# First modulation stage: odd tiles of the adaptive weights go to TensorE, even tiles stay on VectorE; input and matrices are loaded in one run per partition, the matrices last

## The reference, cut to what matters

```python
mod = (jax.nn.silu(c.astype(jnp.float32)) @ ada_w[l].astype(jnp.float32)
       + ada_b[l].astype(jnp.float32))[:, None, :]
shift1, scale1, gate1, shift2, scale2, gate2 = jnp.split(mod, 6, axis=-1)

h = rms_norm(x, norm1_g[l]) * (1.0 + scale1) + shift1
z = (h.astype(in_dtype) @ w_in[l]).astype(jnp.float32)
```

## Time and profile before

| | |
|---|---|
| time, median of 3 executions | 2176.35 us (2171.0 to 2176.57) |
| the profiled execution | 2177.08 us |
| its span | 2175.2 us |
| TensorE (PE) busy | 1868.7 us, 86% |
| VectorE (DVE) busy | 1485.5 us, 68% |
| ScalarE (ACT) busy | 1016.9 us, 47% |
| GpSimd (POOL) busy | 437.7 us, 20% |
| mean granted TensorE clock | 0.94 |

### The profile page before, as it was taken

How to read it: one execution, slowest core, us unless ns; L and a number is a source line. 1 busy time by engine, 2 the same in 40 slices (tenths; PEclk the granted TensorE clock), 3 DMA queues, 4 the chain that set the end, 5 groups by cost and what they waited for, 6 DMA issues and landing times. The chain is left out here.

```text
span 2175.2 us, 33251 instructions
## 1 busy us (share of the span) xinstructions
PE 1868.7 (86%) x12082; PEld 1393.0 (64%) x12082; DVE 1485.5 (68%) x2609; ACT 1016.9 (47%) x2046; POOL 437.7 (20%) x457
## 2 busy tenths in 40 slices
PE   4974897878888778777799989889999999779998
PEld 4842887644432222222279988678998988668997
DVE  6675554777767667666466675766677787676666
ACT  2444212445544444444355554467665545335554
POOL 0010220045454434434200000002231330210000
PEclk8987998889999999999999999699999999889999
DMA  8861001399999999999955655035555655224553
GB/s 327 292 219 34 3 3 41 109 406 420 419 419 420 419 420 419 420 420 420 386 185 184 192 172 202 1 116 176 191 181 177 192 175 174 93 84 160 186 189 98
DMA packets 104385, 497.31 MB, mean 229 GB/s; under 512 B 11856, under 2 KB 17232, under 8 KB 71376
## 3 DMA queue, kind: packets, MB, share of 16 engines
q1 hardware_dynamic: 66064, 225.41, 31.2%
q0 software_dynamic: 36864, 268.45, 29.8%
q10 hardware_dynamic: 1344, 1.96, 0.3%
HBM read 494.73 MB, written 1.05 MB: 228 GB/s over the span
## 5 line engine op out<-in xcount | busy, mean ns | idle before, releaser
L247 PE MATMUL ps<-srcs,wh 128*128 128x512 f32 x2064 | 743.2, 402 | 32.1 <-DVE srcs L261 20.4
L1874 PE MATMUL ps<-row,diag 128*128 128x512 f32 x1024 | 502.3, 626 | 121.4 <-ACT diag L1957 121.2
L249 PE MATMUL ps<-srcs,wl 128*128 128x256 f32 x2064 | 583.5, 283 | 0.0
L229 DVE TENSOR_TENSOR wl<-ring,wh 128x1024 fp32r<-128x1024 f32 x362 | 452.3, 1252 | 123.0 <-ACT wh L223 121.8
L247 PEld LDWEIGHTS ps<-srcs,wh 128*128 128x128 f32 x2064 | 392.5, 190 | 127.7 <-issue 35.9
L1874 PEld LDWEIGHTS ps<-row,diag 128*128 128x128 f32 x1024 | 184.0, 195 | 430.1 <-ACT diag L1957 271.7
L2050 DVE CUSTOM_DVE_ANT_0 row<-row,h_tok 128x1024 f32<-128x1024 f32 x256 | 313.8, 1226 | 198.6 <-DMA row<-in_peer_uv,experts 190.7
L223 ACT ACTIVATE wh<-ring 128x1024 fp32r<-128x1024 f32 x362 | 379.1, 1052 | 66.3 <-PE ps L249 43.5
L249 PEld LDWEIGHTS ps<-srcs,wl 128*128 128x128 f32 x2064 | 396.3, 192 | 2.0 <-issue 1.9
L1811 POOL DMA_INDIRECT row<-in_peer_uv,experts x256 | 281.5, 1100 | 393.1 <-PE ps L1874 342.9
L1950 ACT ACTIVATE acts<-dots 128x1 f32<-128x1 f32 x256 | 51.8, 202 | 329.4 <-DVE dots L2050 328.9
(11 more groups left out here) (503 smaller groups left out, 2083.0 us busy)
## 6 DMA issues: line engine op xcount, KB each, us to landing
ring<-in_stream SPq DMA_DIRECT2D x378, 512.0 KB, 3.7
alpha<-in_ada_late SPq DMA_DIRECT2D x12, 512.0 KB, 5.1
beta<-in_ada_late SPq DMA_DIRECT2D x10, 512.0 KB, 6.0
kappa<-in_ada_late SPq DMA_DIRECT2D x10, 512.0 KB, 5.9
row<-in_peer_uv,experts POOLq DMA_INDIRECT x256, 15.4
bias<-in_attn_bias SPq DMA_DIRECT2D x8, 256.0 KB, 5.0
w<-in_cmp_w SPq DMA_DIRECT2D x1, 2048.0 KB, 7.5
xT<-in_xT SPq DMA_DIRECT2D x1, 1024.0 KB, 15.9
```

The source lines that it names most:

```text
L229: nc.vector.tensor_tensor(wl[:, n % PAIRS, :], ring[:, tile % RING, :], wh[:, n % PAIRS, :].bitcast(F32), ALU.subtract).then_inc(tiles_fre ...
L247: nc.tensor.matmul(out, wh[:, n, cols], source.rearrange("p a t -> p (a t)"), start=start, stop=stop, skip_group_check=True)
L249: return nc.tensor.matmul(out[:, 0:S], wl[:, n, cols], source[:, 0, :], start=False, stop=stop, skip_group_check=True)
L1874: last = nc.tensor.matmul(y_part(t, half), diag[:, s % DIAGS, :], row[:, s % ROWS, D + half * 512:D + (half + 1) * 512], start=(slot == 0) ...
```

## The change

Even tiles stay with DVE, which adds them into `acc` as before, now four a half instead of eight. Odd tiles go to TensorE: `odd_tile` multiplies each block of 128 columns of the ring's tile (stationary) by the one column `cs[k]`, and accumulates into column `at` of bank 0. `even_tiles` adds the sum of `acc` over partitions to the same columns. TensorE's order is: odd tiles 1, 3, 5, 7, mean square, even tiles of half 0, odd tiles 9, 11, 13, 15, even tiles of half 1. The counters `even_added` and `odd_added` take the place of `tiles_freed` in this stage, and the refills wait for the two in turn. DVE's scale of the mean square now stands ahead of tile 12, and the reciprocal ahead of tile 14. The ones matrix is set by POOL. `xT` and `mats` are laid out by the host so that each partition reads one run; `mats` without the ones matrix is loaded by SP behind tile 17, and TensorE waits for it in a later stage.

```diff
--- before.py
+++ after.py
@@ -66,7 +66,7 @@
 NVEC = _at
 
 
-MATS = ["ident", "ones", "blockones", "rotate"]
+MATS = ["ones", "ident", "blockones", "rotate"]
 for _d in range(2):
     MATS += [f"strict{_d}", f"upto{_d}"]
 HALF = P // 2
@@ -315,8 +315,9 @@
             dve.wait_ge(inverted, 1)
 
         cs = sb("cs", [P, KT])
+        mats_in = sem("mats_in")
         with ExitStack() as tmp, stage() as (block, (c_ready, columns, v, squared, summed, scaled, root, inverted, vecs_in,
-                                                     x_in, mats_in, *_)):
+                                                     x_in, ones_in, even_added, odd_added, *_)):
             acc = sb("acc", [P, T_ADA // KT, D], where=tmp)
             first = take(T_ADA)
 
@@ -324,13 +325,16 @@
             def _(sp):
                 for i in range(RING):
                     sp.dma_start(ring[:, i, :], A["stream"][i]).then_inc(loaded[i], 16)
-                sp.dma_start(xT[:, :, :], A["xT"].rearrange("(k p) t -> p k t", p=P)).then_inc(x_in, 16)
-                refill(sp, first, T_ADA)
+                sp.dma_start(xT[:, :, :], A["xT"]).then_inc(x_in, 16)
+                for i in range(T_ADA):
+                    sp.wait_ge(odd_added if i % 2 else even_added, i // 2 + 1)
+                    sp.dma_start(ring[:, i % RING, :], A["stream"][i + RING]).then_inc(loaded[i % RING], 16)
+                    if i + RING == T_ADA + AHEAD - 1:
+                        sp.dma_start(mats[:, 1:, :], A["mats"][:, 1:, :]).then_inc(mats_in, 16)
 
             @block.scalar
             def _(act):
                 act.dma_start(vecs[:, :], A["vecs"]).then_inc(vecs_in, 16)
-                act.dma_start(mats[:, :, :], A["mats"].rearrange("m p n -> p m n")).then_inc(mats_in, 16)
                 act.wait_ge(vecs_in, 16)
                 nc.scalar.activation(cs[:, :], vec_all("c"), ACT.Silu).then_inc(c_ready, 1)
                 act.wait_ge(x_in, 16)
@@ -343,23 +347,25 @@
 
             @block.vector
             def _(dve):
+                dve.sem_inc(tiles_freed, T_ADA)
                 dve.wait_ge(c_ready, 1)
-                for i in range(T_ADA):
+                for i in range(0, T_ADA, 2):
                     total, k, slot = acc[:, i // KT, :], i % KT, i % RING
-                    if i == T_ADA - 3:
+                    if i == T_ADA - 4:
                         dve.wait_ge(summed, 1)
                         nc.vector.tensor_scalar(rstd[:, :], ps[:, 7, 0:S], 1.0 / D, NORM_EPS, ALU.mult, ALU.add
                                                 ).then_inc(scaled, 1)
+                    if i == T_ADA - 2:
+                        dve.wait_ge(root, 1)
+                        nc.vector.reciprocal(rstd[:, :], rstd[:, :]).then_inc(inverted, 1)
                     dve.wait_ge(loaded[slot], 16 * (i // RING + 1))
                     if k == 0:
                         nc.vector.tensor_scalar(total, ring[:, slot, :], cs[:, 0:1], None, ALU.mult
-                                                ).then_inc(tiles_freed, 1)
+                                                ).then_inc(even_added, 1)
                     else:
-                        dve.wait_ge(tiles_freed, i)
+                        dve.wait_ge(even_added, i // 2)
                         nc.vector.scalar_tensor_tensor(total, ring[:, slot, :], cs[:, k:k + 1], total, ALU.mult,
-                                                       ALU.add).then_inc(tiles_freed, 1)
-                dve.wait_ge(root, 1)
-                nc.vector.reciprocal(rstd[:, :], rstd[:, :]).then_inc(inverted, 1)
+                                                       ALU.add).then_inc(even_added, 1)
                 low(dve, T_ADA)
                 dve.wait_ge(columns, 1)
                 nc.vector.tensor_tensor(mod[:, 0:T_ADA], ps[:, 0, 0:T_ADA], vec_all("ada_b")[:, 0:T_ADA], ALU.add
@@ -370,16 +376,35 @@
 
             @block.tensor
             def _(pe):
-                def column(u):
-                    pe.wait_ge(tiles_freed, KT * (u + 1))
+                def odd_tile(i):
+                    pe.wait_ge(loaded[i % RING], 16 * (i // RING + 1))
                     for j in range(KT):
-                        last = nc.tensor.matmul(ps[:, 0, u * KT + j:u * KT + j + 1], acc[:, u, j * P:(j + 1) * P],
-                                                mat("ones")[:, 0:1], start=True, stop=True)
+                        at = i // KT * KT + j
+                        last = nc.tensor.matmul(ps[:, 0, at:at + 1], ring[:, i % RING, j * P:(j + 1) * P],
+                                                cs[:, i % KT:i % KT + 1], start=(i == 1 and j == 0), stop=False,
+                                                skip_group_check=True)
+                    last.then_inc(odd_added, 1)
+
+                def even_tiles(u):
+                    pe.wait_ge(even_added, KT // 2 * (u + 1))
+                    for j in range(KT):
+                        at = u * KT + j
+                        last = nc.tensor.matmul(ps[:, 0, at:at + 1], acc[:, u, j * P:(j + 1) * P], mat("ones")[:, 0:1],
+                                                start=False, stop=True, skip_group_check=True)
                     return last
-                pe.wait_ge(mats_in, 16)
+                pe.wait_ge(c_ready, 1)
+                for i in range(1, KT, 2):
+                    odd_tile(i)
+                pe.wait_ge(ones_in, 1)
                 mean_square(pe, squared, summed)
-                column(0)
-                column(1).then_inc(columns, 1)
+                even_tiles(0)
+                for i in range(KT + 1, T_ADA, 2):
+                    odd_tile(i)
+                even_tiles(1).then_inc(columns, 1)
+
+            @block.gpsimd
+            def _(pool):
+                nc.gpsimd.memset(mat("ones"), 1.0).then_inc(ones_in, 1)
 
         late_in = [sem(f"late_in{i}") for i in range(LATE_RING)]
         late_used = sem("late_used")
@@ -1115,6 +1140,7 @@
 
             @block.tensor
             def _(pe):
+                pe.wait_ge(mats_in, 16)
                 pe.wait_ge(squared, 1)
                 for pair in range(2):
                     for q in range(4):
@@ -2807,8 +2833,8 @@
                "lam_re": cols(f["s5_lam_re_2"]), "lam_im": cols(f["s5_lam_im_2"]),
                "log_dt": cols(np.repeat(f["s5_log_dt_2"][0], 64))}
     out["vecs"] = np.concatenate([vectors[n] for n in VEC], axis=1)
-    out["xT"] = f["x"][0].T
-    out["mats"] = constant_matrices()
+    out["xT"] = f["x"][0].T.reshape(KT, P, S).transpose(1, 0, 2)
+    out["mats"] = constant_matrices().transpose(1, 0, 2)
     out["lora_up"] = np.concatenate([f["w_decay_up"][0].transpose(1, 0, 2), f["a_gate_up"][0].transpose(1, 0, 2)], 0)
     out["g_up"] = f["g_up"][0]
     out["subkeys"] = np.stack([f["peer_sub_keys1"][0].T, f["peer_sub_keys2"][0].T], axis=1)
```

## The result

Over 20 executions each, the changed kernel takes 2177.05 us and the kernel before 2172.93 us (medians; 2172.6 to 2182.6 and 2168.7 to 2176.6). The ratio is 1.0021 with a 95% interval of 1.0012 to 1.0030, so the change makes this kernel slower by 4.6 us (2.6 to 6.5). The median of before that the forecast started from, 2176.35, was of three executions; with twenty it is 3.4 us lower. So the forecast of 2182.5 must be read as its shift, +6.2, against a measured shift of the medians of +4.1.

A forecast was written before the change was run, and what follows sets the result against it. First stage's end was bound by DMA, DVE's adds, one one-column group, then `mod`; after the change by TensorE: 47.2 us, less 3.2 lift, plus tail and stalls, `mod` at 44.4, +6.2. 2176.35 + 6.2 = 2182.5 us; range 2174 to 2188.

The forecast's parts named there:

- What ends the stage: First stage: TensorE, without a gap from 6.2 to about 44 us, ends it; `mod` at 44.4 against 38.16, +6.2 us.
- Prices at 1.2 GHz: TensorE in the first stage: one-column weight loads 0.214 us apart, 3.42 us a group; mean square 6.83 us.
- Start and stalls: TensorE in the first stage: begins at 6.2 us; odd 7 waits 0.2 us for its tile, waits between groups 0.
- The lift: TensorE's clock at 2.4 GHz for one stretch of 3.4 us, brought by the mean square, saving 3.2 us.
- The rival with two stretches: Half the mean square falls into the first 2.4 GHz stretch, a second follows: 3.2 us less, 2179.3; chance 0.10.
- What a measurement can tell: Whole-kernel time: about 0.3%, 6.5 us, can be told from no change; chances 0.06 faster, 0.51 same, 0.43 slower.
- Matrices and `xT`, "nothing": First-stage loads: matrices last on SP and xT in one run per partition change nothing; xT lands before odd 7 (16.5).
- Waits on SP and DVE: First stage: refills waiting in turn and DVE's new waits cost nothing; tile 17 lands near 37.5, split before 44.
- The DMA share under 0.9 from 17 to 44 us: Sign that the forecast is right: DMA engines get idle time in the first stage that costs nothing.
- POOL's memset: Ones matrix set by POOL in the first stage: 0 to 0.40 us, wanted at 20 us, so nothing.
- A clock that one-column work raises: Rival: four odd tiles in a row bring TensorE to 2.4 GHz early, stage end at 32.6, 2170.8 us; chance 0.13.

The follow-up runs named there:

- the divided mean square: The changed kernel with the mean square in two halves, even group 0 and odd 9 between them: ratio 1.0048 to before; profiled executions 2172.11 and 2184.26 us.

## Why the prediction was right or wrong

- **What ends the stage** was right. TensorE is last, DVE waits 4.98 us for it, and nothing behind gave the shift back: 3.0 us at `mod`, 3.6 at 123 us, 4.1 of medians.
- **Prices at 1.2 GHz** were right. Without any lift the forecast's sum is 44.4 + 3.2 = 47.6, with 0.2 of stall in it. The execution of the divided mean square that never left 1.2 GHz has no stall, and its `mod` is at 47.48.
- **Start and stalls** were right within 0.3 us: first odd tile 5.98 (6.2 said), 0.28 us of wait at odd 7 (0.2 said), the mean square from 20.07 (20.1 said).
- **The lift** is the term of the sum that failed. I gave it one stretch of 3.4 us, 3.2 us saved, since that was the one stretch of the kernel before. It lasted 6.8 us in both profiles and saved 6.4: the forecast's 44.4 less another 3.2 is 41.2, which is the measured `mod`. The rival with two stretches had the shift at `mod` right (+3.0), and I had given it 0.10. Its reason was that more of the mean square falls into the first stretch. In the changed kernel that was 2.1 us of it (22.9 to 25.0), and in its second profile 1.4 us (24.4 to 25.8), against 1.2 before. The other explanation would be that TensorE went on working behind it, where it fell idle at 27.8 before. The two profiles of the version with all tiles on VectorE speak against that: in the first, 0.6 us of the mean square ran at 2.4 GHz and the clock fell 3.4 us after its rise, at 23.9; in the second it was 1.3 us, and the clock stayed up for 6.8 us, until 25.5, although TensorE was idle from 21.8:

```profile
19.90:21.70 1.80, 1.80 (x17) 1.75 (x16) 1.59 (x3) 0.00 (x0) 0.00 (x0) 1.00 1.01 405
21.80:25.40 3.60, 0.00 (x0) 0.00 (x0) 3.50 (x4) 0.42 (x1) 0.00 (x0) 1.00 1.02 406
```

  So the rival's reason fits these profiles and continued work is not needed. No run varied the one with the other held.
- **What a measurement can tell** failed too, and it set the chances. I took 6.5 us as the least shift that can be told from none, put the forecast of +6.2 just under it, and gave most weight, 0.51, to no measurable change. Twenty executions of each kernel told 4.6 us from none, with an interval of some 2 us to either side: the kernel is slower, as the sum said and the weights did not. A lift of the right size would not have helped, since it makes the forecast +3.0.
- **The number.** The stated 2182.5 was 5.5 us too high: the start, 2176.35, by 3.4, the lift by 3.2, and against these 1.1 us of the measured shift lie behind `mod`, where the forecast had none. The range was wide enough for all of it. That this 1.1 us took some of the error back was luck.
- **Matrices and `xT`, "nothing"**, was right for the changed kernel only in the sense that nothing waited for them. What they freed was the ring: 4.9 us beside the sharing, 5.5 us without it. My sum had used that silently, by letting tile 7 land at 16 us when it had to be near 21 with the old loads. A term that I had booked at nothing was the one gain in the change.
- **Waits on SP and DVE** were right: tile 16 was split from 33.9 and tile 17 from 36.2 on, the scale of `rstd` came at 25.2, all ahead of need. The DMA share under 0.9 from 17 to 44 us, named as a sign, did not come: it was 0.98 from 17 to 25 us, 0.05 from 25 to 30, and 0.98 again until 41. Nothing waited for that idle time.
- **POOL's memset** took 0.20 us, inside the bounds, from 0.73 us on.
- **A clock that one-column work raises** did not happen: 14 us of it from 6 to 20 us left the loads 0.21 us apart. The Trainium skill ("TensorE: Matmul & The Clock Gate", Part 1) ties the release of the throttle to activity; these runs disagree where the activity is one column per weight load.

## What to carry to other kernels

Before work moves to an engine that looks idle, price it at the state in which the engine will be: here a group cost 3.4 us, not 1.8, because products of one column did not bring TensorE to 2.4 GHz. Share work with a second engine only as long as the first engine still finishes last: four tiles were free, eight cost 8.6 us. And test the parts of a change alone; this one held a gain of 5.5 us under a larger loss, and its loads with all tiles on VectorE, or with only the early odd ones on TensorE, beat the kernel before by 5 to 9 us (ratios 0.9975 to 0.9958) and the changed one by more.

## What was not expected of the hardware

- A mixture of 1.75 us of 256-column products and 1.76 us of one-column products ran at 2.4 GHz for 14 us (6.3 to 20.6) without a fall, but the same mixture did not bring the clock back from 1.2 GHz in 24 us (28.4 to 52.4).
- The clock stayed at 2.4 GHz with TensorE idle from 21.8 to 25.5 us in one profile of the version with all tiles on VectorE; in the other it fell at 23.9, 1.0 us after TensorE's last product.
- One kernel's executions can differ by two whole stretches at 2.4 GHz in the same place: `mod` at 41.5 and at 47.5 us with the divided mean square.
- The window view prints a granted clock of 1.00 as long as there is no record of it. In the divided mean square's second execution it did so through all of the first stage, 41 us of work on TensorE with its one-column loads 0.21 us apart. Only that spacing told.
